# Encoder layer on one Trainium2 core: the side gate's product as seven products of half matrices, grouped with the second MLP product

## The reference, cut to what matters

```
    h2 = rms_norm(x, norm_mlp_g)
    x = x + jnp.square(jax.nn.relu(h2 @ w_mlp1)) @ w_mlp2

    hp = rms_norm(x, norm_ple_g)
    x = x + jax.nn.sigmoid(hp @ w_ple_gate) * (p @ w_ple_proj)
```

## Time and profile before

| | us |
|---|---|
| median of three runs | 2573.27 (2572.18 to 2575.65) |
| profiled execution | 2573.2, span 2571.7 |
| PE busy in the span | 2544.0 (99%) |
| DVE busy | 1520.3 (59%) |
| ACT busy | 1066.8 (41%) |
| POOL busy | 246.3 (10%) |

### The profile page before, as it was taken

How to read it: one execution, slowest core, us unless ns; L and a number is a source line. 1 busy time by engine, 2 the same in 40 slices (tenths; PEclk the granted TensorE clock), 3 DMA queues, 4 the chain that set the end, 5 groups by cost and what they waited for, 6 DMA issues and landing times.

```text
span 2571.7 us, 40372 instructions
## 1 busy us (share of the span) xinstructions
PE 2544.0 (99%) x15483; PEld 2321.4 (90%) x15483; DVE 1520.3 (59%) x2254; ACT 1066.8 (41%) x1731; POOL 246.3 (10%) x405
## 2 busy tenths in 40 slices
PE   7999999999999999999999999999999999999999
PEld 6889888898888988889888888899999999999887
DVE  5545454563554644546443354987888867677843
ACT  5554245442444434444343244633333333333622
POOL 4001000100001000010010011011111300000000
PEclk9999999999999999999999999999999999999999
DMA  3122121221212212122162233244434862542022
GB/s 118 34 26 76 44 75 26 35 75 37 73 34 35 75 46 65 34 35 75 60 243 98 100 111 124 70 149 135 147 126 138 301 213 91 168 148 82 25 64 68
DMA packets 196583, 236.41 MB, mean 92 GB/s; under 512 B 13896, under 2 KB 167056, under 8 KB 196400
## 3 DMA queue, kind: packets, MB, share of 16 engines
q0 software_dynamic: 34576, 138.78, 17.1%
q1 hardware_dynamic: 160768, 95.05, 13.1%
q10 hardware_dynamic: 1056, 0.14, 0.0%
HBM read 168.73 MB, written 65.02 MB: 91 GB/s over the span
## 4 chain that ended last, share of the span: by engine, by line
PE 92%; DVE 4%; issue 2%; DMA 1%; ACT 1%; SPq 0%; POOL 0%; DVEq 0%; ACTq 0%
PE banks L1124 17%; PE banks L1126 17%; PE banks L1125 17%; PE banks L1520 5%; PE banks L1522 5%; PE banks L1521 5%; PE banks L1451 4%; PE banks L1449 4%; PE banks L1450 4%; PE banks L1248 2%; PE banks L1354 1%; PE banks L1353 1%; PE banks L1355 1%; PE banks L1229 1%; PE banks L1327 1%
## 5 line engine op out<-in xcount | busy, mean ns | idle before, releaser
L1124 PE MATMUL banks<-act_hi,w_hi 128*128 128x512 f32 (+1 forms) x2208 | 823.1, 373 | 0.9 <-DVE w_lo L2169 0.8
L1126 PE MATMUL banks<-act_hi,w_lo 128*128 128x512 f32 (+1 forms) x2208 | 783.6, 355 | 0.0
L1125 PE MATMUL banks<-act_lo,w_hi 128*128 128x512 f32 (+1 forms) x2208 | 782.2, 354 | 0.0
L1126 PEld LDWEIGHTS banks<-act_hi,w_lo 128*128 128x128 f32 x2208 | 416.5, 189 | 60.1
L1124 PEld LDWEIGHTS banks<-act_hi,w_hi 128*128 128x128 f32 x2208 | 417.6, 189 | 54.0 <-DVE w_lo L2169 1.8
L1125 PEld LDWEIGHTS banks<-act_lo,w_hi 128*128 128x128 f32 x2208 | 418.3, 189 | 49.3
L1520 PE MATMUL banks<-op,ring 128*128 128x320 f32 x896 | 277.3, 309 | 2.8 <-issue 2.1
L1521 PE MATMUL banks<-op,ring 128*128 128x320 f32 x896 | 276.9, 309 | 0.0
L1522 PE MATMUL banks<-op,ring 128*128 128x320 f32 x896 | 276.9, 309 | 0.0
L1827 ACT ACTIVATE work<-banks 128x512 f32<-128x512 f32 (+4 forms) x204 | 101.3, 503 | 292.9 <-PE banks L1126 292.9
L2169 DVE TENSOR_TENSOR w_lo<-w_raw,w_hi 128x1024 fp32r<-128x1024 f32 x110 | 130.6, 1187 | 78.1 <-ACT w_hi L1607 75.8
(11 more groups left out here) (368 smaller groups left out, 4681.5 us busy)
## 6 DMA issues: line engine op xcount, KB each, us to landing
w_raw<-in_w_in_dram SPq DMA_DIRECT2D x76, 512.0 KB
operand_scratch<-work POOLq DMA_DIRECT2D x112, 320.0 KB, 2.7
op_f<-operand_scratch POOLq DMA_DIRECT2D x28, 1280.0 KB, 6.5
w_raw<-in_w_mlp_dram SPq DMA_DIRECT2D x48, 512.0 KB, 5.5
work<-gate_scratch POOLq DMA_DIRECT2D x16, 640.0 KB, 5.4
gate_scratch<-work POOLq DMA_DIRECT2D x15, 640.0 KB, 3.3
raw<-in_w_mlp_dram SPq DMA_DIRECT2D x16, 512.0 KB, 5.7
work<-weight_scratch POOLq DMA_DIRECT2D x12, 640.0 KB, 5.8
```

The source lines that it names most:

```text
L1124: nc.tensor.matmul(out, wh, rh, start=first and k == 0, stop=False, skip_group_check=True)
L1125: nc.tensor.matmul(out, wh, rl, start=False, stop=False, skip_group_check=True)
L1126: mm = nc.tensor.matmul(out, wl, rh, start=False, stop=k == kt - 1, skip_group_check=True)
```

## The change

The side gate's product is done as a fifth group of seven half-matrix products behind the four of the second MLP product. The steps run on without a break, 28 more (`GATES` = 140), in the order 1, 2, 6, 4, 5, 7, 3. The operands are halves of x itself, or sums of them made by DVE (`gate_sums`); the norm's vector goes into the weights instead (`weights_scaled`, 16 ACT instructions of 512 columns on the raw weights in place). The bank results are copied or added into gate rows 8 to 15 of `work`: by ACT for products 1 and 2 (`gate_copied`), by DVE for the others (`gate_evacuated`). Four of the seven additions of squares go to POOL (1280 columns each), and twelve of the sixteen multiplications of half gate rows by the root (640 columns each); DVE does the other four behind the last step. The transposes of p move behind the second, third and fourth step of product 3, and all eight projections behind the last step, one row at a time, with the row before it transposed behind it. Each row has a staging row of its own. The rows go in the order 4 to 7, 0 to 3.

```diff
@@ PE
-            projected(0)
-            for j in range(KT):
-                n = gate_slab(j)
-                if j == KT - 1:
-                    projected(1)
-                for c in range(3):
-                    ready(n, c)
-                    steps(w_slot(n), c, 0, KT, KT, act_hi, act_lo).then_inc(mm_done, 1)
...
+            for i in range(KT):
+                n = N_P0 + i // 4
+                for c in range(3):
+                    if i % 4 == 0 and c == 0:
+                        pe.wait_ge(w_split, n + 2)
+                    if i == 0:
+                        pe.wait_ge(p_low, 6 if c else 5)
+                    else:
+                        pe.wait_ge(pp_mul, 3 * (i - 1) + c + 2)
+                    steps(w_slot(n), c, 0, 2, 2, p_hi, p_lo, column=lambda k: 4 * k + i % 4).then_inc(pp_done, 1)
+                if i:
+                    for c in range(3):
+                        transposed_y(i - 1, c)
@@ ACT
+                if g == -3:
+                    weights_scaled(0, 0)
+                if g == 1:
+                    weights_scaled(1, 0)
+                if g == 3:
+                    weights_scaled(1, 1)
+                if g == 4:
+                    weights_scaled(0, 1)
+                if 1 <= g <= 8:
+                    gate_copied(h - 1)
+                if h + 2 < GATES:
                     v_weight_high(h + 2)
...
+                elif q < 2 and o < 7 * GROUPS + 7 and o != 33:
+                    gate_high_made(o, q)
...
+                if 0 <= g < 4:
+                    square(4 + g)
...
+            p_high_part(4)
+            for p in range(4):
+                gate_sigmoid(p, 1, op_sum, 10 + p + 2)
+            split_high(N_P1, w_slot(N_P1))
@@ DVE
+            GATE_SUMS = {1: (0,), 2: (1,), 3: (2,), 4: (3,), 5: (4,), 6: (5,), 9: (6,), 10: (7,), 16: (8, 9)}
+            GATE_LOWS = {-3: (28, 0), -2: (28, 1), 1: (29, 0), 2: (29, 1), 6: (30, 0), 7: (30, 1), 9: (31, 0), 10: (31, 1),
+                         13: (32, 0), 14: (32, 1), 18: (33, 0), 19: (33, 1), 21: (34, 0), 22: (34, 1)}
...
             dve.wait_ge(n_r, 3)
+            for p in range(4):
+                dve.wait_ge(v_evac, gate_evac(3, p))
+                row = gate_half(p, 1)
+                v_.tensor_tensor(row, row, r_bc[:, 640:T], ALU.mult).then_inc(op_sum, 1)
+            dve.wait_ge(v_done, GATES + 1)
+            split_low(N_P1, w_slot(N_P1))
@@ POOL
+            for q in range(4, KT):
+                pool.wait_ge(sq_ple, q + 2)
+                pool.sem_inc(pool_passed, 1)
+                pool.wait_ge(acc_ple, q)
+                nc.gpsimd.tensor_tensor(x_next[:], x_next[:], work[:, 10 + q % 2, :], ALU.add).then_inc(acc_ple, 1)
```

More of the change, by code:

```diff
@@ L494, in encoder, with staging, y_bank @@
         STATES, OUTPUTS = states_to(NT), outputs_to(NT)
+        ROWS_P = (4, 5, 6, 7, 0, 1, 2, 3)
         def gate_row(j):
[L498 to L508, removed]
+            return work[:, 8 + j, :]
+        def staging(i):
+            return stage[:, 2 + i, :]
+        def y_bank(i, c):
+            return (3, 4, 5)[c] if i == KT - 1 else 5 + c
         PAIRS = FF // (2 * P)
@@ L1386, in _, with column_sum @@
                 whole(n + 1, (N_C1 + 1) % 2, 4, ob_hi, ob_lo, lambda c: pe.wait_ge(c_low, 5))
-            def column_sums(row):
-                for c, (t0, tw) in enumerate(CHUNKS):
-                    mm = nc.tensor.matmul(bank[3 + c][:, 0:tw], ones[:], row[:, t0:t0 + tw],
-                                          start=True, stop=True, skip_group_check=True)
-                return mm
+            def column_sum(c, row):
+                t0, tw = CHUNKS[c]
+                return nc.tensor.matmul(bank[c][:, 0:tw], ones[:], row[:, t0:t0 + tw],
+                                        start=True, stop=True, skip_group_check=True)
             def out_tile(i, e, last):
@@ L2034, in _, with root_of @@
                     op_high_made(0, 1)
+            def root_of(c):
+                t0, tw = CHUNKS[c]
+                A(r_bc[:, t0:t0 + tw], bank[c][:, 0:tw], ACT.Ln, bias=eps[:], scale=1.0 / D).then_inc(n_ln, 1)
             def p_high_part(i):
@@ new lines, in gate_copied, with gate_sigmoid @@
+            def gate_copied(h):
+                kg, p, m = second(h)
+                act.wait_ge(v_done, h + 2)
+                if m == 1:
+                    act.wait_ge(acc_ple, 4)
+                else:
+                    act.wait_ge(acc_ple, KT)
+                dst = gate_half(4 + p, 1) if m == 1 else gate_half(p, 0)
+                A(dst.rearrange("p (j n) -> p j n", j=2), banks[:, 2 * p:2 * p + 2, 0:320], ACT.Copy).then_inc(c_copied, 1)
+            def gate_sigmoid(j, side, after, count):
+                act.wait_ge(after, count)
+                g = gate_half(j, side)
+                A(g, g, ACT.Sigmoid).then_inc(pg_sig, 1)
@@ L2057, in _ @@
+            TAIL = SECOND - 28
+            for h in range(GATES):
+                g = h - SECOND
+                if g == -3:
[9 more added lines that the diff above has]
+                if h + 2 < GATES:
                     v_weight_high(h + 2)
@@ new lines, in _, with y_out @@
+            p_high_part(4)
+            for p in range(4):
+                gate_sigmoid(p, 1, op_sum, 10 + p + 2)
+            split_high(N_P1, w_slot(N_P1))
+            act.wait_ge(v_done, GATES + 1)
+            def y_out(i, c):
+                t0, tw = CHUNKS[c]
+                act.wait_ge(yt_done, 3 * i + c + 2)
+                A(staging(i)[:, t0:t0 + tw], bank[y_bank(i, c)][:, 0:tw], ACT.Copy).then_inc(yt_read, 1)
+            for i in range(KT - 1):
+                for c in range(3):
+                    y_out(i, c)
```

502 lines of the change are left out of this document (253 added, 249 removed).

## The result

| | us |
|---|---|
| before, median of 6 runs | 2572.8 (2572.18 to 2575.65) |
| after, median of 6 runs | 2590.68 (2588.19 to 2593.55) |
| ratio | 1.0068, 95% interval 1.0055 to 1.0081 |
| profiled execution of after | 2593.55, span 2592.0 |

The changed kernel is slower by 0.7%; the forecast was 2571.0 in 2564 to 2580. The profiled execution is the slowest of the six, 2.9 us above the median; what follows is made against it, 20.3 us of span above that of before.

The account below looks back on a forecast made before the run. PE was taken as the bound (92% of the chain): 2373.7 + 189.7 - 11.7 of matmuls + 12.0 of gaps + 2.8 of end + 3.0 of clock = 2569.5 span; execution 1.5 more, forecast 2571.0 us, range 2564 to 2580.

Parts of the forecast that it names:

- The gain of 11.7: PE's matmuls: eight slabs of 13.79 us (110.3) become 28 steps of 3.52 (98.6), 11.7 us less.
- Rival (d): The 28 steps don't hold the 3.52 pace; each 0.4 late eats the gain, 2582 us; chance 0.06.
- Wait 1: PE before step 8, product 6: waits 4.9 us for DVE's operand behind 21.7 us of ACT work and 11.6 behind it.
- if ACT were on time it would still be about 1.9: Lower end of the wait before step 8, with ACT's high half of step 7 at 2431.2.
- POOL's additions: Four 1280-column additions of squares, taken at 3.6 us each; up to 3.4 is hidden, so 0.4 us of waiting.
- rival (b): POOL is dear: additions of 5.7 us and slower root products give 2578.1, about 2582 with full clock loss; chance 0.14.
- rival (c): POOL and DVE exclude each other during the four additions: 8.8 us more, 2579.8, slower; chance 0.08.
- it was slowed by 0.3, not held: Evidence against POOL/DVE exclusion: a DVE weight split took 1527 ns instead of 1225, ending inside POOL's first instruction.
- Wait 2: PE before the second projection row: 5.2 us for DVE's late first product, 8.8 us after the last p transpose.
- The small waits: PE: 0.5 at step 0, 0.5 in two places further on, 0.5 before the last transposes; 1.5 us.
- The clock: PE's lower clock of 1.2 GHz after the two long waits: 3.0 us taken, between nothing and 8.2.
- The end: From PE's end to the span's end, ACT's copy and the store: 2.8 us, as in the kernel before.

Follow-up runs that it names:

- e7_noscale: Changed kernel with three fills in place of each of POOL's four additions of squares, and the 16 weight scalings cut to 8 columns each; 2583.95 us.
- e2: Changed kernel with the eight later root multiplications on DVE instead of POOL, two behind each of steps 23 to 26; 2585.97 us.
- e5: Changed kernel with DVE's last four root multiplications, their sigmoids and the second projection weights' splits moved behind projection rows instead of ahead of the first; 2583.28 us.
- e16_tt_pieces: Changed kernel with DVE's weight split at 27.7 us cut into four 256-column pieces and GpSimd's two scalings there in the additions' two-input form; 2598.57 us, one execution.
- e9_scalar: Changed kernel with each of POOL's four additions of squares replaced by a scaling of the same 1280 columns by a column vector; 2590.93 us.
- e13_short: Changed kernel with one short fill in place of each of POOL's four additions and the 16 weight scalings cut to 8 columns; 2581.57 us.

## Why the prediction was wrong, by its own steps

- **The gain of 11.7** held. From 2454.56 (step 8) to the end of step 23 (2517.15 - 2.17) are 60.4 us: 16 steps of 3.52, 2.15 of column sums, and 1.5 of lower clock make 60.0. Rival (d) is out.
- **Wait 1** came out near its size as long as nothing is held, 5.67 measured with fills of 3.6 us, 5.3 predicted with the additions at 3.6, but in part by luck, for its make-up was wrong. The step "if ACT were on time it would still be about 1.9" left out two things: the squares and their additions, not only the scalings, stand ahead of product 6's operand (4.56 in e7_noscale), and step 8's weight sums wait for PE's step 5 (2.8 when both are short).
- **POOL's additions** took 2.98 alone, where 3.6 was taken; rival (b) is out. The Trainium skill's figure (GPSIMD Engine Reference, section 3.1) had given an estimate of 2.8, the nearest of the three.
- **The step that failed** is the weighing of rival (c): "it was slowed by 0.3, not held". The row was read for the ratio of two durations (1527 to 1225) instead of for the moment at which the instruction could have begun, and it belongs to another form: a scaling of 1024 columns, which holds for 1 us, while an addition holds nearly to its end. So the sum had nothing in it for the exclusion; measured, the gaps are 20.95 instead of 12.0, 8.95 more. The rival had been given 0.08. That its price was 8.8 is luck: it counted the four additions alone, which cost PE 4.35 us of waiting; another 4.75 stood beside the eight later root multiplications (2.17, 0.37 and 3.05 became 0.84 in e2), for which it had nothing.
- **Wait 2**: 5.2 predicted, 4.96 measured, and the terms behind it were those named (e5).
- **The small waits** of 1.5: 5.97 in the changed kernel (0.38, 2.17, 0.37 and 3.05), and 0.38 and 0.84 with the multiplications on DVE. With fills and e2's edit together the gaps would be 0.39 + 5.67 + 0.84 + 4.95 = 11.9, the 12.0 of the sum; that kernel was not run.
- **The clock** is the second error. 3.0 was taken between nothing and 8.2, two waits and one past stretch as the measure. There were four stretches, 8.5 us. Even rival (c) at 2579.8 has only 3.0 in it.
- **The end** is the third: "+ 2.8" was carried over from before, although the change moves all eight rows' stores to the end, one each 4.6 us, and the last two together. It was 8.4. No term of the sum looked at the stores.

The sum with the measured sizes: 2569.5 + 8.95 + 5.5 + 5.6 = 2589.6 for the span, against 2592.0.

The Trainium skill (SBUF — State Buffer, section "Who interferes with whom") says that a DVE instruction with two SBUF inputs contends with a GpSimd one that reads SBUF, and not with one that only writes it. That is what the additions, the scalings and the fills show. The same page (section "SBUF: two separate sides") says that whichever starts first has the shared ports for its whole instruction. That holds within some 0.1 us for the additions and within 0.6 for scalings of 1280 columns, and not for the scaling of 1024, which let DVE through after 0.97 and 0.98 us of 2.85.

## What to carry to other kernels

Before work is given to GpSimd to relieve VectorE, ask whether GpSimd's instruction reads SBUF and whether VectorE's own beside it have two inputs there; where both are so, as here, price it as time of both engines, 2.98 us of POOL against 1.48 on DVE itself. When one row speaks against a rule that would turn the sign of a forecast, compare its form and shape, and work out from its end when it really began, before the rule is given a chance of 0.08. And a change that moves the last stage has a new tail: count the bytes that are stored after the last matmul.

## What the runs showed of the hardware that I had not expected

- How long GpSimd's TENSOR_SCALAR holds a two-input VectorE instruction back depends on its width: 0.98 us of 2.85 for 1024 columns, 2.9 of 3.45 for 1280. A TENSOR_TENSOR holds nearly to its end with 1024 columns (e16_tt_pieces) and with 1280.
- POOL waits too, and VectorE can get an instruction in first: the three scalings behind one another in e9_scalar took 16.09 us instead of 10.6 (three of 3.54), and an instruction of 0.68 that began 1.1 us into the first (2426.45) was not held. So a recorded start of POOL is not always the moment from which it holds.
- From the fifth group on, in the profiled executions of all these kernels, the clock fell in or within 1.5 us behind every wait of PE of 3.0 us or more, behind about half of those of 2.8 us (0.79 from 2451 to 2459 in after; 1.00 from 2440 to 2460 in e5_tail and e13_short), once behind one of 2.17 (e7_noscale) and not behind those of 0.8.
